# Per-map counting of scores, maxima and exponentials in the even layer's two-map attention

## The reference

```
def one_block(args):
    causal = (t0 + jnp.arange(QBLK))[:, None] >= kpos[None, :]
    s1 = einsum('bqhd,bkhd->bhqk', q1b, k);  s2 = the same of the second half
    p1 = softmax(where(causal, s1, -inf));   p2 = softmax(where(causal, s2, -inf))
    return einsum('bhqk,bkhd->bqhd', p1 - lam * p2, v)
```

## Time and profile before

| | us |
|---|---|
| median of 3 runs | 2710.94 |
| lowest and highest of them | 2702.87, 2714.01 |
| the profiled execution, own time | 2701.26 |
| its span, first to last instruction | 2699.5 |
| TensorE busy in the span | 2307.3 |
| VectorE, ScalarE busy | 1019.7, 589.6 |
| two-map items 0 to 15, in the span | about 2019 to 2114 |

### The profile page before, as it was taken

One profiled execution on the slowest core, in us unless ns is written; L12 is line 12 of the kernel. 1 busy time (PEld: TensorE's weight loads), 2 busy tenths in 40 slices (PEclk: granted clock), 3 DMA queues, 4 the chain that ended last, 5 costly groups with the idle time before them and its releaser, 6 DMA issues. The chain is left out here.

```text
span 2699.5 us, 29938 instructions
## 1 busy us (share of the span) xinstructions
PE 2307.3 (85%) x11804; PEld 1514.6 (56%) x11804; DVE 1019.7 (38%) x1782; ACT 589.6 (22%) x1229; POOL 249.5 (9%) x295
## 2 busy tenths in 40 slices
PE   4999987699785897888888888885998989799998
PEld 2877657589674333333333333333775767688775
DVE  3677526545745010101011010115744554563443
ACT  4442213244411000000000000002332421223311
POOL 4223326500110000000000000000000000000000
PEclk8999988599887999999999999997998999899999
DMA  6123636354410999999999999994220131221030
GB/s 218 58 86 121 215 110 180 82 148 118 152 69 24 417 417 417 417 416 416 417 417 418 417 418 418 416 416 161 90 78 31 32 117 63 100 94 63 32 133 31
DMA packets 209222, 569.87 MB, mean 211 GB/s; under 512 B 62584, under 2 KB 97377, under 8 KB 175713
## 3 DMA queue, kind: packets, MB, share of 16 engines
q1 hardware_dynamic: 202104, 559.45, 54.5%
q0 software_dynamic: 2496, 8.40, 1.0%
q10 hardware_dynamic: 4521, 0.64, 0.1%
HBM read 540.14 MB, written 28.31 MB: 211 GB/s over the span
## 5 line engine op out<-in xcount | busy, mean ns | idle before, releaser
L1897 PE MATMUL ps_gate_up<-expert_ring_early,one_expert_columns 128*64 128x512 f32 x512 | 252.0, 650 | 87.6 <-DMA expert_ring_early<-in_moe_w_up_dram 73.8
L1897 PE MATMUL ps_gate_up<-expert_ring,one_expert_columns 128*64 128x512 f32 x512 | 233.4, 610 | 47.1 <-DMA expert_ring<-in_moe_w_up_dram 47.0
L1964 DVE TENSOR_TENSOR hidden_tokens<-silu_gate,ps_gate_up 64x512 f32<-64x512 f32 x64 | 42.5, 690 | 609.6 <-ACT silu_gate L1943 609.1
L1898 PE MATMUL ps_gate_up<-expert_ring_early,one_expert_columns 128*64 128x512 f32 x512 | 252.8, 651 | 0.0
L1898 PE MATMUL ps_gate_up<-expert_ring,one_expert_columns 128*64 128x512 f32 x512 | 234.0, 611 | 0.0
L1877 PE MATMUL ps_down<-expert_ring,hidden_columns 128*64 128x512 f32 x512 | 226.6, 595 | 0.0
L1878 PE MATMUL ps_down<-expert_ring,hidden_columns 128*64 128x512 f32 x512 | 226.6, 595 | 0.0
L1897 PEld LDWEIGHTS ps_gate_up<-expert_ring_early,one_expert_columns 128*64 128x64 f32 x512 | 73.4, 149 | 249.0 <-issue 249.0
L1897 PEld LDWEIGHTS ps_gate_up<-expert_ring,one_expert_columns 128*64 128x64 f32 x512 | 69.9, 141 | 193.0 <-issue 193.0
L1877 PEld LDWEIGHTS ps_down<-expert_ring,hidden_columns 128*64 128x64 f32 x512 | 67.5, 137 | 130.1 <-issue 127.9
L846 DVE SCALAR_TENSOR_TENSOR conv_out<-conv_in,tap_columns,conv_out 128x770 f32<-128x770 f32 (+1 forms) x96 | 124.2, 1294 | 3.4
(11 more groups left out here) (506 smaller groups left out, 4625.9 us busy)
## 6 DMA issues: line engine op xcount, KB each, us to landing
expert_ring<-in_moe_w_down_dram SPq DMA_DIRECT2D x64, 2048.0 KB, 19.5
expert_ring_early<-in_moe_w_gate_dram SPq DMA_DIRECT2D x32, 2048.0 KB, 16.1
expert_ring_early<-in_moe_w_up_dram SPq DMA_DIRECT2D x32, 2048.0 KB, 20.6
expert_ring<-in_moe_w_gate_dram SPq DMA_DIRECT2D x32, 2048.0 KB, 22.5
expert_ring<-in_moe_w_up_dram SPq DMA_DIRECT2D x32, 2048.0 KB, 24.2
win_ring<-in_gdn_w_in_dram SPq DMA_DIRECT2D x16, 1024.0 KB, 7.9
late_mod_ring<-in_w_mod_dram SPq DMA_DIRECT2D x16, 1024.0 KB, 5.4
stream_raw<-in_w_in_even_dram SPq DMA_DIRECT2D x16, 1024.0 KB, 5.2
```

The source lines that it names most:

```text
L1897: mm(psA[LO, c], xe[:, e, k], gu[s0][:, j, cols], start=(k == 0), stop=(k == KC - 1))
L1898: last = mm(psA[HI, c], xe[:, e, k], gu[s1][:, j, cols], start=(k == 0), stop=(k == KC - 1))
L1964: nc.vector.tensor_tensor(hid[HI, c % 2], sg[HI, c % 2], psA[HI, c], ALU.mult).then_inc(hidden, 1)
```

## The change

The three semaphores now count maps. `upto(n)` is the number of maps up to and with item n: 2 for each of the items 0 to 15, 1 for each after (in the odd layer 1 for all, so its counts are as before). `scores(n)` waits before map a for the exponential of map a of item n-1, `maximum(n)` for the scores of map a, `exponential(n)` for the maximum of map a. Each of the three counts up behind every map. `finish_probs(n)`, the first two biased items (16 and 17) and the end of the loop wait for all maps of the item in question.

```diff
+    upto = lambda n: sum(MAPS[gi] for gi, _, _ in ITEMS[:n + 1])
@@ scores
-                    if maps == 2:
-                        if n:
-                            pe.wait_ge(exped, n)
-                    elif even and n < GI + 2:
-                        pe.wait_ge(exped, GI)
+                    if even and GI <= n < GI + 2:
+                        pe.wait_ge(exped, upto(GI - 1))
                     elif biased(n):
                         pe.wait_ge(bias_done, n - 2 - GI + 1)
-                    elif n >= 2:
-                        pe.wait_ge(exped, n - 1)
+                    elif maps == 1 and n >= 2:
+                        pe.wait_ge(exped, upto(n - 2))
                     for a in range(maps):
+                        if maps == 2 and n:
+                            pe.wait_ge(exped, upto(n - 2) + a + 1)
...
-                    last.then_inc(scored, 1)
+                        last.then_inc(scored, 1)
@@ exponential
-                    act.wait_ge(maxed, n + 1)
...
+                        act.wait_ge(maxed, upto(n - 1) + a + 1)
+                        nc.scalar.activation(pr[:, c, a, 0:W], src, ACT.Exp, bias=st[:, c, a, 0:1], accum_out=st[:, c, a, 1:2]).then_inc(exped, 1)
@@ maximum
-                    dve.wait_ge(scored, n + 1)
                     if biased(n):
+                        dve.wait_ge(scored, upto(n))
...
+                        dve.wait_ge(scored, upto(n - 1) + a + 1)
+                        nc.vector.tensor_reduce(st[:, n % DEEP, a, 0:1], src, AX_X, ALU.max, negate=True).then_inc(maxed, 1)
@@ finish_probs
-                    dve.wait_ge(exped, i + 1)
+                    dve.wait_ge(exped, upto(i))
```

More of the change, by code:

```diff
@@ L2277, in turn_mixed @@
                         pe.wait_ge(taken, N)
-                        pe.wait_ge(exped, N)
+                        pe.wait_ge(exped, upto(N - 1))
                     for t in range(LT):
@@ L2355, in exponential @@
                         src = sc[:, n % 2, 0:W] if biased(n) else bank[4 + (a if maps == 2 else n % 2)][:, 0:W]
-                        last = nc.scalar.activation(pr[:, c, a, 0:W], src, ACT.Exp, bias=st[:, c, a, 0:1], accum_out=st[:, c, a, 1:2])
-                    last.then_inc(exped, 1)
+                        act.wait_ge(maxed, upto(n - 1) + a + 1)
+                        nc.scalar.activation(pr[:, c, a, 0:W], src, ACT.Exp, bias=st[:, c, a, 0:1], accum_out=st[:, c, a, 1:2]).then_inc(exped, 1)
                 def keep_probs(i):
@@ L2490, in maximum @@
                     W, maps = (t + 1) * P, MAPS[gi]
-                    dve.wait_ge(scored, n + 1)
                     if biased(n):
+                        dve.wait_ge(scored, upto(n))
                         if n >= GI + 2:
-                            dve.wait_ge(exped, n - 1)
+                            dve.wait_ge(exped, upto(n - 2))
                         i = n - GI
@@ L2502, in maximum @@
                         src = sc[:, n % 2, 0:W] if biased(n) else bank[4 + (a if maps == 2 else n % 2)][:, 0:W]
-                        last = nc.vector.tensor_reduce(st[:, n % DEEP, a, 0:1], src, AX_X, ALU.max, negate=True)
-                    last.then_inc(maxed, 1)
+                        dve.wait_ge(scored, upto(n - 1) + a + 1)
+                        nc.vector.tensor_reduce(st[:, n % DEEP, a, 0:1], src, AX_X, ALU.max, negate=True).then_inc(maxed, 1)
                 def finish_probs(i):
```

## The result

The median of seven runs is 2692.66 us, that of seven runs of the kernel before 2705.47. The ratio is 0.9946, with an interval from 0.9929 to 0.9962: faster by 0.54% (0.38 to 0.71%), 14.6 us of 2705. One run of the changed kernel took 7657.66 us at a mean granted clock of 0.36, where all others have about 0.93; the ratio leaves it out. The profiled execution has a span of 2689.3 us against 2699.5 before. The changed kernel measured again against eleven other runs of before gave 0.9938 (0.9919 to 0.9957).

A forecast was written before the change was run, and what follows sets the result against it. TensorE was taken as the bound, with 9.5 us of waits for exponentials. Restarts 6.7, plus 4.1 and 1.2 from the clock, made 12.0 us off 2710.9: forecast 2699, range 2687 to 2711.

The forecast's parts named there:

- restart of item 1: TensorE resumes after item 0's exponential, still behind ScalarE's table load: 1.05 us gained, 0.37 idle stays.
- restart before item 3: TensorE's idle behind item 2's exponentials, in a round without a chunk, goes entirely: 2.12 us gained.
- restarts before 6, 11, 14: TensorE's idles of 0.65, 1.23 and 0.64 us behind exponentials go in full: 2.52 us gained.
- item 9: Maxima stand behind VectorE's weight split; only one maximum and one exponential go: 0.60 us gained, 2.47 idle stays.
- item 16: Waits for both maps of item 15; the first exponential may start one maximum earlier: 0.41 us gained.
- first slow stretch: Lower TensorE clock after item 0: stays but is shortened, 1.2 us gained, between bounds 0 and 3.9.
- second slow stretch: Lower TensorE clock over item 3's scores and chunk, begun in the idle before them: goes, 4.1 us gained.
- third slow stretch: Lower TensorE clock after the idle before item 9: stays, 0 gained, between bounds 0 and 2.9 us.
- Extra waits: 15 more waits on TensorE between maps: taken as 0, upper bound 1.9 us at 0.13 each.
- B: Rival: only the restarts gain, the clock falls elsewhere among the items for as long; -6.7 us, 2704; chance 0.20.
- C: Rival: all lower-clock periods among items 0 to 16 nearly go; -17.6 us, 2693; chance 0.18.
- D: Rival: map 0's scores still wait, from late counting or splits ahead of every maximum; -1 us, 2710; chance 0.06.
- E: Rival: slower, as the clock also stays low from 2045 to 2072; +17 us, 2728; chance 0.06.

The follow-up runs named there:

- The two part experiments: The changed kernel with only exponentials counted per map (2706.83 us), and with only scores and maxima counted per map, TensorE waiting for the whole item before (2700.57 us).
- the fillers: Three unused products added ahead of item 0: 2694.31 us on the changed kernel, 2681.55 us (ratio 0.9906) with the splits one round later as well.

## Why the prediction was right

The forecast was 12.0 us less, 2699 for the median, in a range from 2687 to 2711. The ratio gives 14.6 less, and the median is 2692.66. Of the 6 us between 2699 and 2692.66 the level of before makes up 5.5: its median was 2710.94 over the three runs that the prediction had, and is 2705.47 over seven. By the steps of the prediction, read in the item starts of the two timelines:

| step | predicted | measured |
|---|---|---|
| restart of item 1 | 1.05 | 1.06 |
| restart before item 3 | 2.12 | 2.31 |
| restarts before 6, 11, 14 | 2.52 | 3.25 |
| item 9 | 0.60 | 0.46 |
| item 16 | 0.41 | 0.51 |
| first slow stretch | 1.2 | 1.07 |
| second slow stretch | 4.1 | 4.13 |
| third slow stretch | 0 | 0.19 |
| the other items | 0 | 0.12 |
| sum | 12.0 | 13.1 |

*The waits* fell from 9.5 to 2.9, by 6.7 us, and the two that stay stand where the prediction put them: 0.25 before item 1 (0.37 predicted) and 2.60 before item 9 (2.47). The two part experiments priced the links at 2.3 and 4.4. "None before items 3, 6, 11, 14, 16" held, item 3 with a margin of 0.05, where 0.2 had been worked out.

*The second slow stretch* went for the reason given; filling the idle in the kernel before gave 4.1 from item 3 to item 4, and 3.9 in the stage. *The first* was shortened as bounded, from a rough halving between two lengths; that this hit was luck as much as method, since the prediction had no cause for that stretch, and none was found. *The third* followed the idle of 2.60, and both went when the split was moved.

*The missed term* is 0.24 us at each of items 6, 11 and 14, 0.19 at item 3 and 0.10 at item 16, 1.0 in all, of a difference of 1.1. The prediction took the idle in brackets for the gain, and wrote that 9.5 us were all that the waits could give. But a product that follows without a wait begins before the modelled end of the one ahead. Before, the products of L2267 begin at 2053.51 and item 6 at 2054.99, 1.48 later, of which the profile calls 0.65 idle; after the change the same two are 0.59 apart:

```profile
2053.51 0.83 PE L2267 MATMUL even_bank<-residual,even_token_work 128*128 128x128 f32 x6
```

```profile
2051.45 0.83 PE L2267 MATMUL even_bank<-residual,even_token_work 128*128 128x128 f32 x6
2052.04 0.42 PE L2244 MATMUL even_bank<-even_mask_parts,even_ident_rounded 128*128 128x384 f32 x1
```

The gain is 0.89, not 0.65. At items 1 and 9, where a wait is left, there is nothing of this: 1.06 us came of 1.17 less idle, and 0.46 of 0.47.

*The part behind the stage* was put at nothing: its items were to start earlier by the sum and no more. The profiles show 3.6 us there, mostly the clock in the odd layer. The ratio's interval, 10 to 19 us, can't tell 13.1 from 16.7.

*Extra waits* cost nothing that shows. The scores of item 7, with a wait more, go from mask to mask in 1.46 us (2058.21 to 2059.67 after the change), and both maps take 2.94; before, the pair took 2.95. The prediction had bounded a wait between the maps at one covered weight load, 0.13 us. There was no such cover to lose: the weight load of the second map's mask starts with its product in both kernels, first before, then after the change:

```profile
2062.66 0.19 PEld L2244 LDWEIGHTS even_bank<-even_mask_parts,even_ident_rounded 128*128 128x128 f32 x1 [0.76 <-issue]
2062.67 0.50 PE L2244 MATMUL even_bank<-even_mask_parts,even_ident_rounded 128*128 128x512 f32 x1
```

```profile
2059.67 0.19 PEld L2244 LDWEIGHTS even_bank<-even_mask_parts,even_ident_rounded 128*128 128x128 f32 x1 [0.76 <-issue]
2059.67 0.50 PE L2244 MATMUL even_bank<-even_mask_parts,even_ident_rounded 128*128 128x512 f32 x1
```

The Trainium skill ("TensorE: Matmul & The Clock Gate", section "Architectural detail") says that TensorE's queue can pull weight loads ahead of running products. At this place neither trace shows it.

*Rivals.* B, the restarts alone, would have been 6.7 of 13.1. C came true in the experiments, not in the change: its 17.6 needs the idle before item 9 gone, and with that and the fillers the stage gained 21.4. D and E left no trace. The whole gain of 14.6 us (10 to 19) holds the 12.0. It stands just past 0.5%, the side to which 0.42 was given, and not within it, the likelier side with 0.52; the interval holds both, and the stage's 13.1 are 0.48%.

*The clock from one execution to the next.* In the stage nothing differed: 81.31 and 81.30 us in the two profiles of the changed kernel. Ahead of it the slow stretches did move. The same 14 products took 6.74 us in the first execution (246.03 to 252.77) and 3.76 in the second (245.53 to 249.29). These are 3.0 of the 6.9 us by which item 0 came earlier in the second. The granted clock was 0.66 and 1.00:

```profile
244.00:254.00 10.00, 9.63 (x40) 5.94 (x41) 6.03 (x11) 0.17 (x1) 3.32 (x3) 0.66 0.64 185
```

```profile
244.00:254.00 10.00, 9.76 (x56) 6.88 (x56) 5.94 (x11) 0.79 (x2) 3.03 (x3) 1.00 0.60 185
```

The Trainium skill ("TensorE: Matmul & The Clock Gate", Part 1) says that the sampling that sets the clock runs freely and isn't aligned with the kernel's start. The rows ahead of the stage agree with it; that the stage's own clock would differ by execution, as the prediction took from it, two profiles don't show.

*Open:* what brings the clock down right after item 0, and why 0.65 and 1.23 us of idle did not do so in the kernel before, while in other kernels 0.43, 1.09 and 1.23 were followed by a slow stretch. Also why the same 2.77 us of idle in the odd layer were followed by one in five profiles of thirteen.

## What to carry to other kernels

Where several pieces of an item pass through a chain of engines, count by piece, but only look for a gain in the rounds where the waiting engine has nothing else to do: the same change was worth 13.1 us with uncovered rounds and 0.5 with a chunk in each. An idle of TensorE can cost more than its length: before item 3, 2.1 us of idle cost 3.9 more in the granted clock, and filling it with unused products got those back. Its length alone doesn't tell whether it will, as the 2.77 us in the odd layer show. Look at what stands ahead of the first short instruction of a chain in its engine's list: moving a split of 3.5 us (1.22 and 2.29) behind two short maxima gained another 5.5 us in the stage.

## What the runs showed that was not expected

- A restart of TensorE that goes away altogether gains 0.1 to 0.24 us more than the idle the profile shows, because the next product then overlaps the modelled end of the last (0.89 for 0.65, 1.48 for 1.23, 0.88 for 0.64, 2.31 for 2.12, 0.51 for 0.41).
- A slow stretch can hide a wait: with the clock held up in item 1, 0.43 us of waiting for VectorE's split came into view before item 3, and another slow stretch after it; the stage stayed at 81.2 us.
- The same idle of 2.77 us, ahead of the same products, was followed by the lower clock in five profiles and by the upper in eight. It was worth 2.8 us, outside everything that the change touches.
- The part of the program ahead of the stage, equal in code, ended anywhere between 2015.8 and 2026.6 us, nearly as much as the change is worth, with slow stretches at other places even for one program; the stage itself repeated to 0.01 in its two profiles.
